# The weighted selection of a pair of experts, turned by 32x32 blocks on VectorE instead of by TensorE

## The chip, the cores and the metric

The kernel runs on one core of one Trainium2 chip. Its time is the device time of one launch in microseconds (us). Engines are named as the profile names them: PE is TensorE (PEld its weight loads), DVE is VectorE, ACT is ScalarE, POOL is GpSimd, SP is SyncE, which here only issues the loads of weights.

## What is computed

A trunk of four layers over 256 tokens of width 1024. Each layer has a token mixer (gated DeltaNet, differential attention, gMLP, DeltaNet again) and then a mixture of 16 experts of which every token takes two. The change lies in the experts alone:

```
for i in range(DEPTH):
    ...                                   # mixer, residual, layer norm
    m = grouped_moe(h, w_router, router_bias, e_w1[i], e_w3[i], e_w2[i])
    h = layer_norm(DN_ALPHA * h + m, ...)

def grouped_moe(x, ...):
    scores = sigmoid(t @ w_router)        # top 2 of the best group of 4 -> gates [256, 16]
    for e in range(N_EXPERTS):
        h = silu(t @ w1[e]) * (t @ w3[e]) # 1024 -> 512
        out = out + gates[:, e:e + 1] * (h @ w2[e])
```

All in float32.

## The kernel before

Each engine has one program written by hand, and the programs meet at semaphores; no scheduler moves anything. The experts of a layer are worked off in eight pairs, seven in a hardware loop and the last (`final`) in code of its own. For each expert up to 64 (`CAP`) of its tokens are picked; an expert with more gets extra passes under a branch (`PASSES`, `baton`).

`rank` on DVE gives each token, for each expert, its place among that expert's tokens (`place`), and `route` its gate (`gates`). A selection is a 0/1 matrix of 128 tokens by 64 slots, made by comparing `place` with the slot number `iota`. `sel` picks the tokens of a pair into `x_`; `selg` is the same with the gate in place of the 1 and brings the results back.

One pair on PE, in this order (function `pair` in the tensor block): `up` of expert 0 into bank 2 and of expert 1 into bank 3 (L1851, 32 matmuls each); `turn` of expert 0: `selg` of the first 128 tokens is transposed (L1858) and then the four pieces of `h_` (L1862), all into bank 2; `gather(0)` for the next pair (L1840, 16 matmuls); `turn` of expert 1, with `selg` of the other 128 tokens, into bank 3; `down` of both (L1869); `gather(1)`; and the four matmuls over `selgT` and `y_` that bring the pair's result back (L1968). The last pair has no gathers.

Around it ACT takes silu (L881) of each bank, copies the transposed selection into `selgT` (L891) and the transposed h into `hT` (L892), and copies `y_` (L897). DVE makes `selg` (L1365) and the next pair's `sel` (L1368), four operations of 128x64 each, taken in turn, at the start of the pair; then the product h of silu and the third matrix (L1374) for expert 0 and expert 1; then `pair_x` (L1343) and `pair_x_shift` (L1348), which scale and shift the gathered x; and adds the four banks of the result to H (L1421). At the start of a layer DVE makes the first `sel` (L1353) and both halves of the first `x_` before it enters the pairs. POOL then forms the scaled residual on H in four operations (L555, L561), in the time of the first pair.

What PE waits for, by bank: `free(b, n)` waits until bank b has been drained n times in this pair. DVE's product h counts as the first draining of bank 2 (expert 0) and of bank 3 (expert 1). Before, `free(2, 1)` and `free(3, 1)` stand directly ahead of the two turns.

SP loads the weights of a pair, six times 2 MiB, into a ring of six slots; a slot is loaded again when PE has passed its last reader (`weights_read`, counted up by the first instruction of expert 1's `up`, of expert 0's `turn`, of expert 1's `down` and of `gather(1)`).

## Time and profile before

| | |
|---|---|
| median of 3 runs | 2070.44 us (2067.48 to 2070.73) |
| profiled execution, its own time | 2060.59 us |
| its span | 2058.8 us |
| PE busy | 1866.4 us, 91% |
| DVE busy | 717.8 us, 35% |
| ACT busy | 502.1 us, 24% |
| POOL busy | 160.0 us, 8% |
| mean granted TensorE clock | 0.95 |
| moved by DMA | 504.47 MB, mean 245 GB/s |

The span is what the profiler sees from the first to the last instruction of the one profiled execution; some 1.8 us lie around it. In the rows below, a line of a timeline gives the start and the length in us, the engine, the line of the kernel, the operation, the tile written and the tiles read, their sizes and how many instructions were merged, and in brackets how long the engine stood idle before it and what ended that. "issue" there is time in which the engine waited for nothing that the profile shows.

### The profile page before, as it was taken

How to read it: one execution, taken by the hardware profiler on the slowest of the kernel's cores; microseconds unless marked ns; L12 is line 12 of the kernel's file. 1: busy time of each engine (PE TensorE's matmuls, PEld its weight loads, DVE VectorE, ACT ScalarE, POOL GpSimd, SP SyncE). 2: the span in 40 equal slices, each digit the busy share in tenths (PEclk: the TensorE clock that was granted, in tenths of full speed). 3: DMA queues.
4: the chain of work that ended last, by engine and by line, in shares of the span. 5: the costliest groups of instructions: out<-in, count | busy, mean ns of one | idle time of the engine just before them, and what ended most of it. 6: DMA issues, size and time to landing. Idle time of an engine off the chain costs nothing. (4 is left out here: it accounts for less than half of the span.)

```text
span 2058.8 us, 28401 instructions
## 1 busy us (share of the span) xinstructions
PE 1866.4 (91%) x10562; PEld 1024.9 (50%) x10563; DVE 717.8 (35%) x1433; ACT 502.1 (24%) x1006; POOL 160.0 (8%) x97
## 2 busy tenths in 40 slices
PE   7998979999895889889979998899989988899996
PEld 6867644443663444334434444434438768434442
DVE  2434453332305452223323115232323435443233
ACT  1664211221203111111111001122113845112211
POOL 1112021000300030000020002100002120020000
PEclk9999999999995899999999998999999999999999
DMA  9421159999741257548994424779994320279994
GB/s 353 143 83 64 42 198 408 429 426 400 269 149 41 82 228 293 209 192 368 428 346 152 163 82 169 301 320 426 421 401 146 123 103 3 82 302 428 424 426 176
DMA packets 80952, 504.47 MB, mean 245 GB/s; under 512 B 8195, under 2 KB 12340, under 8 KB 55996
## 3 DMA queue, kind: packets, MB, share of 16 engines
q1 hardware_dynamic: 69808, 488.65, 58.9%
q0 software_dynamic: 2304, 8.39, 1.2%
q10 hardware_dynamic: 8716, 5.66, 1.0%
q8 instruction: 92, 1.51, 0.3%
q14 instruction: 32, 0.26, 0.0%
HBM read 501.62 MB, written 1.06 MB: 244 GB/s over the span
## 5 line engine op out<-in xcount | busy, mean ns | idle before, releaser
L1851 PE MATMUL bank<-ring,work 128*64 128x512 f32 x2176 | 485.3, 604 | 12.0 <-DVE work L1388 6.0
L1851 PEld LDWEIGHTS bank<-ring,work 128*64 128x64 f32 x2176 | 156.0, 139 | 332.1 <-issue 324.7
L1869 PE MATMUL bank<-ring,work 128*64 128x512 f32 x1088 | 245.5, 602 | 7.5 <-ACT work L903 4.6
L1521 PE MATMUL bank<-HT,ring 128*128 128x256 f32 x1024 | 231.7, 386 | 4.3 <-DMA ring<-in_a_w_in 3.3
L1521 PEld LDWEIGHTS bank<-HT,ring 128*128 128x128 f32 x1024 | 198.3, 194 | 41.6 <-issue 11.5
L1529 PE MATMUL bank<-ring,HT 128*128 128x512 f32 x448 | 196.4, 598 | 0.0
L1374 DVE TENSOR_TENSOR work<-bank,work 64x512 f32<-64x512 f32 x64 | 68.1, 1064 | 325.5 <-ACT work L881 325.4
L881 ACT ACTIVATE work<-bank 64x512 f32<-64x512 f32 x64 | 37.7, 589 | 528.5 <-PE bank L1851 528.5
L1840 PE MATMUL bank<-work 128*128 128x128 f32 x1024 | 141.7, 296 | 11.0 <-DVE work L1353 7.2
L1869 PEld LDWEIGHTS bank<-ring,work 128*64 128x64 f32 x1088 | 76.7, 138 | 147.2 <-issue 139.7
L1840 PEld LDWEIGHTS bank<-work 128*128 128x128 f32 x1024 | 129.8, 206 | 36.4 <-issue 27.0
L1529 PEld LDWEIGHTS bank<-ring,HT 128*128 128x128 f32 x448 | 85.8, 193 | 104.3 <-issue 104.3
L1343 DVE TENSOR_TENSOR work<-bank,lncols 128x512 f32<-128x512 f32 x64 | 44.3, 692 | 261.9 <-PE bank L1840 261.9
L1968 PE MATMUL bank<-work 128*128 128x512 f32 x256 | 115.8, 595 | 9.4 <-issue 4.5
L897 ACT ACTIVATE work<-bank 64x512 f32<-64x512 f32 x128 | 75.8, 592 | 183.1 <-PE bank L1869 182.4
L1068 DVE SCALAR_TENSOR_TENSOR work<-bank,convcols,work 128x255 f32<-128x255 f32 x144 | 69.1, 481 | 108.3 <-ACT work L696 104.8
L1421 DVE TENSOR_TENSOR H<-bank,H 128x512 f32<-128x512 f32 x128 | 84.7, 686 | 58.6 <-PE bank L1968 58.3
L1554 PE MATMUL bank<-ring,work 128*128 128x512 f32 x192 | 84.9, 601 | 0.0
L1968 PEld LDWEIGHTS bank<-work 128*128 128x128 f32 x256 | 46.4, 191 | 59.2 <-issue 59.2
L558 POOL TENSOR_TENSOR H<-H,gB 128x1024 f32<-128x1024 f32 x6 | 14.0, 2356 | 751.6 <-PE bank L1512 751.6
L555 POOL TENSOR_TENSOR H<-work,gB 128x1024 f32<-128x1024 f32 x8 | 23.0, 2899 | 574.5 <-DVE work L1348 574.5
L1554 PEld LDWEIGHTS bank<-ring,work 128*128 128x128 f32 x192 | 36.5, 193 | 44.4 <-issue 44.4
(275 smaller groups left out, 1757.0 us busy)
## 6 DMA issues: line engine op xcount, KB each, us to landing
ring<-in_e_w SPq DMA_DIRECT2D x192, 2048.0 KB, 13.2
ring<-in_a_w_in SPq DMA_DIRECT2D x16, 2048.0 KB, 15.6
ring<-in_c_w_in SPq DMA_DIRECT2D x8, 2048.0 KB, 12.5
ring<-in_b_w_in SPq DMA_DIRECT2D x6, 2048.0 KB, 15.3
ring<-in_a_w_out SPq DMA_DIRECT2D x4, 2048.0 KB, 8.0
ring<-in_c_w_out SPq DMA_DIRECT2D x4, 2048.0 KB, 8.1
ring<-in_b_w_out SPq DMA_DIRECT2D x2, 2048.0 KB, 8.2
gB<-in_ln_mix_g POOLq DMA_DIRECT2D x4, 512.0 KB, 4.1
```

Of the source, the lines that this page charges most:

```text
L897: ins = a(y_[CAP * j:CAP * (j + 1), nh * 512:(nh + 1) * 512], bank[b][nh * CAP:(nh + 1) * CAP, :], ACT.Copy)
L1068: ins = v.scalar_tensor_tensor(dst[:, back:SEQ], ps[:, 0:SEQ - back], convcols[:, j, col:col + 1], dst[:, back:SEQ], ALU.mult, ALU.add)
L1343: v.tensor_tensor(sl, bank[g][:, :].rearrange("p (k c) -> p k c", k=4), lncols[:, g_col + 4 * g:g_col + 4 * g + 4].unsqueeze(2).to_broadca ...
L1374: v.tensor_tensor(by_m(h_[j]), bank[b][CAP:, :], sil[j][CAP:, :], ALU.mult).then_inc(drained[b], 1)
L1421: v.tensor_tensor(part(b), bank[b][:, :], part(b), ALU.add).then_inc(drained[b], 1)
L1521: ins = mm(dst[:, 0:SEQ], wt[:, k, n * P:(n + 1) * P], HT[:, k, :], start=k == 0, stop=k == KC - 1)
L1529: ins = mm(dst[:, :], HT[:, k, tt * P:(tt + 1) * P], wt[:, k, :], start=k == 0, stop=k == KC - 1)
L1554: ins = mm(ps[:, :], turned(h, tt), wts[nh][:, h, :], start=h == 0, stop=h == HEADS - 1)
L1840: ins = mm(bank[g][:, k * 2 * CAP:(k + 1) * 2 * CAP], XH[:, tt, (4 * g + k) * P:(4 * g + k + 1) * P], sel[:, tt, :], start=tt == 0, stop=t ...
L1851: ins = mm(bank[b][lo:lo + CAP, :], x[:, k, :], wt[:, k, :], start=k == 0, stop=k == KC - 1, skip_group_check=True)
L1869: ins = mm(bank[b][nh * CAP:(nh + 1) * CAP, :], h[:, m, :], w2[:, m, nh * 512:(nh + 1) * 512], start=m == 0, stop=m == 3, skip_group_check ...
L1968: mm(bank[b][:, :], selgT[:, tt * P:(tt + 1) * P], y_[:, nh * 512:(nh + 1) * 512], start=True, stop=True).then_inc(filled[b], 1)
```

## The change

The selection with gates is no longer made token by slot and transposed by PE. It is made slot by token in blocks of 32, so that a transpose within blocks, which DVE can do, gives `selgT`. For this each quarter of the partitions (32 of them) needs the places and gates of all four quarters. Once per layer 16 copies spread them over the quarters (`spread`, from `placed`, in which `place` and `gates` now lie side by side). In a pair DVE compares `slot_no` with the places (128x256), multiplies by the gates, makes the next `sel` as before (four operations), and transposes by blocks into `selgT`.

PE loses the two transposes of `selg` per pair, ACT the two copies into `selgT`. The wait for h of expert 0, `free(2, 1)`, moves from the turn into the middle of expert 1's `up`; the one for h of expert 1, `free(3, 1)`, moves ahead of the last matmul of `gather(0)`. The count of `sel_ready` is now given by DVE's transpose, and PE waits for it a second time before the last matmuls of the pair.

```diff
+                for a in range(4):
+                    for tb in range(4):
+                        out = spread[Q * a:Q * (a + 1), :, :].rearrange("p q (n t b) -> p t q n b", t=TT, b=4)
+                        ins = v.tensor_copy(out[:, :, :, :, tb], placed[Q * tb:Q * (tb + 1), :, :, a // 2:E:2])
+                ins.then_inc(spread_set, 1)
...
                 def pair(it, final):
-                    for tt in range(TT):
-                        for j in range(2):
-                            ins = v.tensor_scalar(selg[:, tt, CAP * j:CAP * (j + 1)], iota, place[:, tt, bass.ds(it * 2 + j, 1)],
-                                                  gates[:, tt, bass.ds(it * 2 + j, 1)], ALU.is_equal, ALU.mult)
-                            if not final:
-                                ins = v.tensor_scalar(sel[:, tt, CAP * j:CAP * (j + 1)], iota, place[:, tt, bass.ds(it * 2 + (j + 2), 1)], None, ALU.is_equal)
-                    ins.then_inc(sel_ready, 1)
+                    blocks = TT * P // Q
+                    at_b = [spread[:, q, bass.ds(it * blocks, blocks)].unsqueeze(2).to_broadcast([P, blocks, Q]) for q in range(2)]
+                    b3 = selb.rearrange("p (n c) -> p n c", c=Q)
+                    v.tensor_tensor(b3, slot_no.unsqueeze(1).to_broadcast([P, blocks, Q]), at_b[0], ALU.is_equal).then_inc(selb_step, 1)
+                    dve.wait_ge(selb_step, it * 2 + (E * i + 1))
+                    v.tensor_tensor(b3, b3, at_b[1], ALU.mult).then_inc(selb_step, 1)
+                    if not final:
+                        for tt in range(TT):
+                            for j in range(2):
+                                v.tensor_scalar(sel[:, tt, CAP * j:CAP * (j + 1)], iota, place[:, tt, bass.ds(it * 2 + (j + 2), 1)], None, ALU.is_equal)
+                    dve.wait_ge(selb_step, it * 2 + (E * i + 2))
+                    v.transpose(selgT, selb).then_inc(sel_ready, 1)
...
-                        a(selgT[:, j * P:(j + 1) * P], bank[b][:, 0:P], ACT.Copy)
                         a(hT[j], bank[b][:, SEQ:].rearrange("p (m c) -> p m c", m=4), ACT.Copy).then_inc(drained[b], 1)
...
-                        head, tail = up(2 + j, x_[:, :, CAP * j:CAP * (j + 1)], w1, w3, None if j else free)
+                        head, tail = up(2 + j, x_[:, :, CAP * j:CAP * (j + 1)], w1, w3, free, (2, 1) if j else (1, 0))
...
-                    free(2, 1)
-                    head, tail = turn(2, [selg[:, 0, :]], h_[0])
+                    head, tail = turn(2, [], h_[0])
...
-                        gather(0)[1].then_inc(filled[0], 1)
-                    free(3, 1)
-                    turn(3, [selg[:, 1, :]], h_[1])[1].then_inc(filled[3], 1)
+                        gather(0, free)[1].then_inc(filled[0], 1)
+                    else:
+                        free(3, 1)
+                    turn(3, [], h_[1])[1].then_inc(filled[3], 1)
...
+                    pe.wait_ge(sel_ready, it + ((E // 2 + 1) * i + 2))
                     free(2, 3)
```

On DVE, at the entry into the loop of the pairs, from its first operation to the product h of expert 0 (`work` holds both `selg` or its blocks and `sel`; ISA and REGISTER_ALU rows set addresses). Before:

```order
L1365 TENSOR_SCALAR work<-consts_sb,place,gates 128x64
L1368 ISA
L1368 TENSOR_SCALAR work<-consts_sb,place 128x64
...
L1365 TENSOR_SCALAR work<-consts_sb,place,gates 128x64
L1368 ISA
L1368 TENSOR_SCALAR work<-consts_sb,place 128x64
L1370 REGISTER_ALU
L1370 TENSOR_LOAD counts
...
L1374 TENSOR_TENSOR work<-bank2,work 64x128x4
```

After:

```order
L1378 TENSOR_TENSOR work<-consts_sb,spread 128x256
L1379 ISA
L1380 ISA
L1380 TENSOR_TENSOR work<-work,spread 128x256
L1384 ISA
L1384 TENSOR_SCALAR work<-consts_sb,placed 128x64
...
L1384 TENSOR_SCALAR work<-consts_sb,placed 128x64
L1386 STREAM_TRANSPOSE work<-work 128x256
...
L1391 TENSOR_TENSOR work<-bank2,work 64x128x4
```

Four gated selections became two products and a transpose; the four plain ones stand together behind the products, and all of it still precedes the product h.

On PE, from expert 1's up-projection (bank 3) through the two turns, in the loop of the pairs, with the semaphores waited for. Before:

```order
L1851 MATMUL bank3<-ring1,work 64x512
L1851 MATMUL bank3<-ring0,work 64x512
L1851 MATMUL bank3<-ring1,work 64x512
...
L1858 MATMUL bank2<-consts_sb,work 128x128 [waits drained2]
L1862 MATMUL bank2<-consts_sb,work 128x64 x4
L1926 REGISTER_ALU
L1840 MATMUL bank0<-work 128x128 [waits sel_ready]
L1840 MATMUL bank0<-work 128x128 x7
L1858 MATMUL bank3<-consts_sb,work 128x128 [waits drained3]
L1862 MATMUL bank3<-consts_sb,work 128x64 x4
```

After:

```order
L1870 MATMUL bank3<-ring1,work 64x512
L1906 REGISTER_ALU
L1870 MATMUL bank3<-ring0,work 64x512 [waits drained2]
L1870 MATMUL bank3<-ring1,work 64x512
...
L1880 MATMUL bank2<-consts_sb,work 128x64 x4
L1944 REGISTER_ALU
L1859 MATMUL bank0<-work 128x128 [waits sel_ready]
L1859 MATMUL bank0<-work 128x128 x6
L1859 MATMUL bank0<-work 128x128 [waits drained3]
L1880 MATMUL bank3<-consts_sb,work 128x64 x4
```

The two transposes of 128x128 are gone, the wait for bank 2 stands in the up-projection, and the wait for bank 3 inside the gather.

## Rows read from the trace of the kernel before

**Rows 1.** Timeline of PE, a settled pair of layer 0 in the loop.

```profile
344.00 13.95 PE L1851 MATMUL bank<-ring,work 128*64 128x512 f32 x64
357.88 0.33 PE L1858 MATMUL bank<-consts_sb,work 128*128 128x128 f32 x1
358.14 0.46 PE L1862 MATMUL bank<-consts_sb,work 64*128 64x64 f32 x4
358.53 2.05 PE L1840 MATMUL bank<-work 128*128 128x128 f32 x16
360.42 0.27 PE L1858 MATMUL bank<-consts_sb,work 128*128 128x128 f32 x1
360.62 0.46 PE L1862 MATMUL bank<-consts_sb,work 64*128 64x64 f32 x4
```

**Rows 2.** Windows, the next pair: busy by engine, then PEclk, DMA share, GB/s.

```profile
373.44:402.89 29.45, 29.45 (x148) 12.65 (x147) 8.99 (x18) 5.93 (x11) 0.00 (x0) 1.00 1.01 428
```

**Rows 3.** Timeline of DVE, first pair of layer 0.

```profile
277.17 0.69 DVE L1343 TENSOR_TENSOR work<-bank,lncols 128x512 f32<-128x512 f32 x1 [3.87 <-PE bank L1840]
...
281.31 0.31 DVE L1365 TENSOR_SCALAR work<-consts_sb,place,gates 128x64 f32<-128x64 f32 x1
...
281.69 2.86 DVE L1365 TENSOR_SCALAR work<-consts_sb,place,gates 128x64 f32<-128x64 f32 x1
...
287.51 2.34 DVE L1368 TENSOR_SCALAR work<-consts_sb,place 128x64 f32<-128x64 f32 x1
289.76 2.38 DVE L1365 TENSOR_SCALAR work<-consts_sb,place,gates 128x64 f32<-128x64 f32 x1
...
292.34 1.07 DVE L1374 TENSOR_TENSOR work<-bank,work 64x512 f32<-64x512 f32 x1
```

**Rows 4.** Timeline of POOL in the same stretch.

```profile
281.57 5.75 POOL L555 TENSOR_TENSOR H<-work,gB 128x1024 f32<-128x1024 f32 x2 [105.10 <-DVE work L1348]
287.40 4.70 POOL L561 TENSOR_TENSOR H<-H,bB 128x1024 f32<-128x1024 f32 x2
```

**Rows 5.** Timeline of PE, first and last pair of layer 0.

```profile
279.87 14.02 PE L1851 MATMUL bank<-ring,work 128*64 128x512 f32 x64
...
304.22 3.65 PE L1869 MATMUL bank<-ring,work 128*64 128x512 f32 x16 [2.74 <-issue]
...
500.34 8.78 PE L1851 MATMUL bank<-ring,work 128*64 128x512 f32 x32 [2.03 <-issue]
...
510.89 0.33 PE L1858 MATMUL bank<-consts_sb,work 128*128 128x128 f32 x1 [1.11 <-DVE work L1374]
```

**Rows 6.** Two lines by source: shortest/median/longest in ns, first and last start.

```profile
L1130 DVE TENSOR_TENSOR HT<-work,consts_sb x40: 413/424/2556, 158.6 to 1732.4; 128x256 f32<-128x256 f32 x40
...
L1106 DVE COPY egl<-work x8: 171/172/433, 125.6 to 1667.7; 128x8 f32<-128x8 f32 x8
```

**Rows 7.** Timeline of DVE in the settled pair of rows 1.

```profile
351.75 1.07 DVE L1374 TENSOR_TENSOR work<-bank,work 64x512 f32<-64x512 f32 x1 [5.35 <-ACT work L881]
...
358.62 1.07 DVE L1374 TENSOR_TENSOR work<-bank,work 64x512 f32<-64x512 f32 x1 [5.80 <-ACT work L881]
```

**Rows 8.** Timeline of PE and DVE, first pair of layer 3.

```profile
1803.23 13.95 PE L1851 MATMUL bank<-ring,work 128*64 128x512 f32 x64
...
1815.73 1.07 DVE L1374 TENSOR_TENSOR work<-bank,work 64x512 f32<-64x512 f32 x1
```

**Rows 9.** Timeline of POOL and DVE, two places where both work in SBUF.

```profile
159.41 4.83 POOL L584 TENSOR_TENSOR work<-work,angb 128x1024 f32<-128x1024 f32 x2 [14.59 <-ACT work L722]
...
160.51 4.02 DVE L1130 TENSOR_TENSOR HT<-work,consts_sb 128x256 f32<-128x256 f32 x2 [1.11 <-PE bank L1625]
...
310.63 2.77 POOL L543 TENSOR_SCALAR gB<-gB 128x1024 f32<-128x1024 f32 x1 [17.11 <-DMA bB<-in_ln_ffn_b]
...
311.94 0.69 DVE L1348 TENSOR_TENSOR work<-work,lncols 128x512 f32<-128x512 f32 x1
```

**Rows 10.** DMA issues from 358.5 to 360, median us to landing.

```profile
ring<-in_e_w SPq DMA_DIRECT2D x2, 2048.0 KB, 15.0
```

More of the change, by code:

```diff
@@ L59 @@
 C_FOLD = C_IOTA + 2 * CAP
-C_SB = C_FOLD + E
+C_SLOT = C_FOLD + E
+Q = 32
+C_SB = C_SLOT + Q
 C_OH = C_SB
@@ L229, in trunk @@
         tri = K_[:, C_TRI:C_TRI + P]
+        slot_no = K_[:, C_SLOT:C_SLOT + Q]
         fold = K_[:, C_FOLD:C_FOLD + E]
@@ L256, in trunk @@
         rs = sb("rs", [P, 4, TT])
-        gates = sb("gates", [P, TT, E])
-        place = sb("place", [P, TT, PASSES * (E + 2)])
+        placed = sb("placed", [P, TT, 2, PASSES * (E + 2)])
+        place, gates = placed[:, :, 0, :], placed[:, :, 1, 0:E]
+        spread = sb("spread", [P, 2, E // 2 * TT * P // Q])
         counts = ctx.enter_context(nc.sbuf_tensor("counts", [1, E], mybir.dt.int32))
@@ L317, in trunk @@
         logitT = work[:, 6144:6144 + SEQ]
+        selb = work[:, 2304:2560]
         iota2 = K_[:, C_IOTA:C_IOTA + 2 * CAP]
@@ L322, in trunk @@
         pairs = work[:, 8704:9216]
-        sel, selg, selgT = view(2048, TT, 2 * CAP), view(2304, TT, 2 * CAP), work[:, 2560:2816]
+        sel, selgT = view(2048, TT, 2 * CAP), work[:, 2560:2816]
         x_ = view(2816, KC, 2 * CAP)
@@ L357, in trunk @@
         sel_ready = sem("sel_ready")
+        spread_set = sem("spread_set")
+        selb_step = sem("selb_step")
         silu_h = sem("silu_h")
@@ L1304, in route @@
                 own.link(v.reciprocal(rs[:, 2, :], rs[:, 1, :]))
-                own.link(v.tensor_tensor(gates[:, :, :], V3(5), rs[:, 2, :].unsqueeze(2).to_broadcast([P, TT, E]), ALU.mult))
+                own.link(v.tensor_tensor(gates, V3(5), rs[:, 2, :].unsqueeze(2).to_broadcast([P, TT, E]), ALU.mult))
             def rank(i):
@@ L1359, in experts @@
                     pair_x_shift(g)
+                dve.wait_ge(spread_set, i + 1)
                 def pair(it, final):
[L1363 to L1369 removed]
+                    blocks = TT * P // Q
[10 more added lines that the diff above has]
+                    v.transpose(selgT, selb).then_inc(sel_ready, 1)
                     counted = [dve.value_load(counts[0:1, bass.ds(it * 2 + j, 1)], min_val=0, max_val=SEQ) for j in range(2)]
@@ L1834, in experts, with gather @@
                 done(mm(ps[:, 2 * E:3 * E], ones[:, :], mask[1], start=False, stop=True, skip_group_check=True), "rank", i)
-                def gather(g):
+                def gather(g, later=None):
                     for k in range(4):
                         for tt in range(TT):
+                            if later is not None and (k, tt) == (3, TT - 1):
+                                later(3, 1)
                             ins = mm(bank[g][:, k * 2 * CAP:(k + 1) * 2 * CAP], XH[:, tt, (4 * g + k) * P:(4 * g + k + 1) * P], sel[:, tt, :],
@@ L1843, in gather, with up @@
                     return head, ins
-                def up(b, x, w1, w3, later=None):
+                def up(b, x, w1, w3, later=None, then=None):
                     for k in range(KC):
                         if later is not None and k == KC // 2:
-                            later(1, 0)
+                            later(*then)
                         for lo, wt in ((0, w1), (CAP, w3)):
@@ L1857, in turn @@
                     for n, tile in enumerate(columns):
-                        ins = tr(bank[b][:, n * P:(n + 1) * P], tile, ident)
-                        head = ins if n == 0 else head
+                        tr(bank[b][:, n * P:(n + 1) * P], tile, ident)
                     for m in range(4):
@@ L1862, in turn @@
                         ins = tr(bank[b][:, c:c + CAP], h[CAP:, m * P:(m + 1) * P], ident[CAP:, CAP:])
+                        head = ins if m == 0 else head
                     return head, ins
@@ L2043, in constants @@
     c[:, C_CD + E:C_CD + 2 * E] = (other > mine).reshape(1, E)
+    c[:, C_SLOT:C_SLOT + Q] = m // Q * Q % CAP + np.arange(Q)[None, :]
     c[:, C_IOTA:C_IOTA + 2 * CAP] = np.arange(2 * CAP) % CAP
```

## The prediction, made before the changed kernel was run

> **What bounds the kernel now.** I read the page first: PE is by far the busiest engine, so the question is where PE waits and what it does in between. The timeline of PE in a settled pair of the expert loop answers it for the largest part: from 344.00 on every row starts where the last one ended [rows 1], the next pair starts at 373.44 [rows 2], so a pair takes 29.44 us, and PE is never idle in it. So in those stretches the time is the sum of PE's instructions, and whatever leaves PE leaves the time, provided nothing else becomes late. The next view is the one of windows: in such a pair the DMA engines are busy all the time and move 428 GB/s [rows 2]. The six loads of a pair are 6 x 2 MiB = 12.58 MB, so PE and DMA run neck and neck. What is not settled is the first pair of each layer. There the timeline of DVE shows selection instructions of 64 columns that take 2.3 to 2.9 us instead of 0.3 [rows 3], exactly while POOL runs its four operations on H [rows 4]. Before the change nobody pays for that. PE asks for h of expert 0 only at its first transpose.
>
> **What leaves PE.** Two 128x128 transposes per pair. Their cost is the distance to the next start: 358.14 - 357.88 = 0.26 and 360.62 - 360.42 = 0.20, together 0.46 us [rows 1]. Four layers have 28 pairs in the loops: 28 x 0.46 = 12.9. In the last pair of a layer there is no gather between the two turns, and in layer 0 PE waits 1.11 us for h of expert 1 before the second turn [rows 5]. Taking 0.26 away ahead of that wait only lengthens it, so such a pair yields 0.20. I count two layers so, and two with 0.46, since there PE stands still earlier and h is ready: 1.3. Sum: 14.2 us off PE.
>
> **What leaves ACT** (two copies of 128x128 a pair) lies beside PE's work. It brings the copies of hT 0.2 to 0.3 earlier, and PE does not wait for them in a settled pair [rows 1]: nothing.
>
> **What DVE gets in a settled pair.** Four selections with a gate go, two products of 128x256 and one blockwise transpose of 128x256 come. A product of that size takes 0.42 (L1130) [rows 6]. For the transpose no row exists: the nearest is the same 0.42, and I bound it from 0.3 to 1.2. Before the product h of expert 0 at 351.75, 7.75 us into the pair, DVE stood idle for 5.35 [rows 7]: the selection was done 2.4 us in. One us more hides there: nothing. The gather now waits for a signal given after the transpose, some 3 to 4 us into the pair, and comes to it at 14.3: nothing. The wait for h of expert 1 moves in front of the gather's last matmul. The sixteen matmuls take 360.42 - 358.53 = 1.89 [rows 1]; with the 0.26 gained they start 14.27 us into the pair, the last at 16.04. h of expert 1 is ready at 358.62 + 1.07 = 359.69, 15.69 us in [rows 7]: a margin of 0.3 us, nothing, but this is the thinnest place.
>
> **What DVE gets once per layer.** Sixteen copies of 32 partitions between the first selection and the first product of x. DVE stands idle there for 3.87 us, ahead of 277.17 [rows 3]. A copy of eight columns (L1106) takes 0.17 [rows 6]; one after the other that is 2.8, with 0.2 each 3.2. Hidden, by the gather on PE. If they took over 0.3 each, some tenths of a us per layer would show.
>
> **The wait that moves.** This is the term that decides. PE now asks for h of expert 0 not at the turn but in the middle of expert 1's up-projection, after 48 of the 64 matmuls. These take 357.88 - 344.00 = 13.88, so the point lies 10.41 us into the pair. In a settled pair h is ready at 7.75 + 1.07 = 8.8 [rows 7]. In the first pair of layer 0, which PE starts at 279.87 [rows 5], the point falls on 290.28, and DVE starts the product h only at 292.34 and needs 1.07: it is ready at 293.41 [rows 3]. So even with DVE exactly as before PE would stand still for 3.1 us, where it now has 0.4 to spare. In layer 3: 1803.23 + 10.41 = 1813.64 against 1815.73 + 1.07 = 1816.80, again 3.2 [rows 8]. Layers 1 and 2 show the same distances within 0.05. Queued behind this wait is the rest of the up-projection, both turns and everything later in the pair; all of it moves.
>
> How does the new code change DVE's lateness? In the rows, one selection gets through at the end of each POOL operation, and the last waits until the fourth has ended at 292.10 [rows 3, 4]. The first product (comparison with the slots) starts ahead of POOL and runs free. The second, by the gates, must wait for the first and so falls under POOL. It reads two tensors from SBUF. L1130 is such an operation: mostly 0.42, but 2.56 at the longest [rows 6], and two of them together take 4.02 from 160.51, under two POOL tensor_tensor on work that begin at 159.41 [rows 9]. Against it stands L1348 at 311.94, also with two SBUF inputs, 0.69 as elsewhere, in the middle of a POOL operation that begins at 310.63 [rows 9]; but that one is a tensor_scalar, and the four here are tensor_tensor [rows 4]. I go by L1130: the product waits for POOL's first operation. Then four selections follow, one or two per POOL operation, the last one again until about 292.2, then the transpose (0.42), then h (1.07): ready at about 293.8. PE stands still for 3.5 us. Four layers: 14.0. The lower bound is that neither the product nor the transpose waits for POOL: then the fourth selection is through at 289.8 (as the row at 287.51 plus its length would be), h is ready at 291.4, and the stall is 1.1. The upper bound has a transpose of 1.2 that waits too: 4.4.
>
> The Trainium skill (SBUF — State Buffer, "Who interferes with whom") says that a DVE instruction with two SBUF inputs contends with a GpSimd instruction that reads SBUF, and that the one which issues first holds the pair to its end. L1130 agrees, L1348 beside the tensor_scalar does not. By the rule the stall is 3.5 and the time 2073.5; were it wrong here, 1.1 and about 2062.
>
> **The clock.** After an idle stretch the 32 matmuls of an up-projection took 8.78 instead of about 7.1 (idle 2.03 before them), while after 2.74 idle 16 matmuls took the usual 3.65 [rows 5]. The stall is longer than both. I charge 1.7 us in two layers of four: 3.4; bounds 0 and 6.8.
>
> **The loads.** A pair of 28.98 us wants 12.58 MB / 28.98 = 434 GB/s, and 428 was moved with the engines full [rows 2]. If 428 is the ceiling, loads fall back 0.4 us per pair, 2.5 to 3 over a layer. The load issued about 359 lands 15.0 later, at 374 [rows 10], and is wanted by expert 1's up-projection of the next pair, which starts half of 13.88 into it, at 373.44 + 6.94 = 380.4: 6 us in hand, and the stall gives the queue 3.5 more. Nothing, but not certain. The Trainium skill (DMA: Bandwidth & Descriptors) names 435 GB/s as the ceiling of the SBUF side; by it 28.98 us would just be fed.
>
> **Sum**, against the profiled execution's own 2060.6: - 14.2 + 14.0 + 3.4 = 2063.8, that is 3.2 more. That execution is 9.8 below the median of the runs, 2070.4, so the median becomes about 2073.5.
>
> **Rivals.**
> - *A short stall.* Product and transpose slip past POOL: 4 x 1.1 + 1.7 for one fall of the clock - 14.2 = -8.1, time 2062.3. For it: L1348's row. Against: L1130's. 0.17.
> - *No stall worth naming*, PE only loses its transposes: 2056.2. It needs DVE through by 290.3, which no row supports. 0.05.
> - *The moved wait costs more than the transposes* (the slower side): the blockwise transpose takes 1.2 and waits for POOL as well, and PE's clock falls each time: 4 x (4.4 + 1.7) - 14.2 = +10.2, time 2080.6. It decides from a stall of some 3.6 with the clock falling in three layers on. For it: the longest idle stretch in the rows that ended in a fall is shorter than this one. 0.17.
> - *The loads become the bound*: pairs stay at 29.4, so only 1 to 3 us of the 14.2 arrive: about +15, time 2085. For it: full DMA engines. Against: 6 us in hand. 0.05.
>
> **How the numbers follow.** The forecast holds 0.56, around 2073.5, give or take 4 for the clock and for code arriving late at other places (idle rows ended by "issue", as the 2.03 and 2.74 us in [rows 5]; the code of the pair is rearranged). A measurement of this kernel can tell about 0.2%, 4.1 us. Of the forecast's 0.56 some 0.02 lies below -4.1 and 0.20 above +4.1. Faster: 0.17 + 0.05 + 0.02 = 0.24; slower: 0.17 + 0.05 + 0.20 = 0.42; same: 0.34. The range from 2062 to 2081 takes in the short stall and the long one and leaves out the two ends.
>
> **What would show it.** In the trace of the changed kernel: settled pairs of 28.98 us without idle PE; in each first pair an idle stretch of PE about 10.4 us in, released by DVE's product h, 3.5 long in the forecast, 1.1 in the first rival; the gate product of 128x256 at 2.5 to 3 us there and 0.42 elsewhere. Idle PE released by DMA on ring in late pairs would mean the loads. The prediction is wrong if h of expert 0 is ready before PE reaches the middle of the up-projection, or if the settled pair does not shrink by 0.46.

## The result, and the profile after

The changed kernel took 2076.17 us in the median of 20 runs (2065.52 to 2087.28), the kernel before 2065.73 in the median of 20 runs interleaved with them (2056.26 to 2074.73). The ratio is 1.0049, with a 95% interval of 1.0034 to 1.0063. That is 10.1 us more, where the prediction said 3.2 more. The profiled execution of the changed kernel has a span of 2074.2 us and a mean granted TensorE clock of 0.944 (before: 2058.8 and 0.95).

A settled pair in the loop, on the timeline of PE (start and length in us, engine, line, what it writes and reads, how many instructions). It answers to [rows 1]; up is now L1870, the turn L1880, the gather L1859, down L1888, the matmuls that bring the result back L1988:

```profile
769.21 13.95 PE L1870 MATMUL bank<-ring,work 128*64 128x512 f32 x64
783.10 0.46 PE L1880 MATMUL bank<-consts_sb,work 64*128 64x64 f32 x4
783.49 2.05 PE L1859 MATMUL bank<-work 128*128 128x128 f32 x16
785.47 0.46 PE L1880 MATMUL bank<-consts_sb,work 64*128 64x64 f32 x4
785.86 7.09 PE L1888 MATMUL bank<-ring,work 128*64 128x512 f32 x32
...
798.29 1.08 PE L1870 MATMUL bank<-ring,work 128*64 128x512 f32 x4
```

The two transposes of the selection are gone, PE is still never idle, and the pair takes 798.29 - 769.21 = 29.08 us instead of 29.44. No wait on a DMA appears in any pair.

The first pair of a layer, here of layers 0 and 1, on the same timeline. The bracket is idle time before the row and what ended it; these rows answer to the first of [rows 5]:

```profile
278.22 10.77 PE L1870 MATMUL bank<-ring,work 128*64 128x512 f32 x48
292.08 6.54 PE L1870 MATMUL bank<-ring,work 128*64 128x512 f32 x16 [3.09 <-DVE work L1391]
...
736.56 10.52 PE L1870 MATMUL bank<-ring,work 128*64 128x512 f32 x48
750.43 3.65 PE L1870 MATMUL bank<-ring,work 128*64 128x512 f32 x16 [3.35 <-DVE work L1391]
```

After 48 of the 64 matmuls PE stands still until DVE's product h of expert 0 (L1391). The list of PE's waits (total us, times, longest) gives the sum over the four layers:

```profile
PE bank L1870 <- DVE work L1391: 13.1, 4, 3.4
```

Why h is late stands on the timelines of DVE and POOL in the first pair of layer 1 (answering to [rows 3, 4]):

```profile
730.82 3.20 DVE L1364 COPY spread<-placed 32x32 f32<-32x32 f32 x16
734.77 0.69 DVE L1349 TENSOR_TENSOR work<-bank,lncols 128x512 f32<-128x512 f32 x1 [0.75 <-PE bank L1859]
...
738.00 0.41 DVE L1378 TENSOR_TENSOR work<-consts_sb,spread 128x256 f32<-128x256 f32 x1
738.57 2.86 DVE L1380 TENSOR_TENSOR work<-work,spread 128x256 f32<-128x256 f32 x1 [0.15 <-DVE work L1378]
741.35 7.60 DVE L1384 TENSOR_SCALAR work<-consts_sb,placed 128x64 f32<-128x64 f32 x4
748.88 0.43 DVE L1386 STREAM_TRANSPOSE work<-work 128x256 f32<-128x256 f32 x1
749.34 1.04 DVE L1391 TENSOR_TENSOR work<-bank,work 64x512 f32<-64x512 f32 x1
...
738.26 5.91 POOL L562 TENSOR_TENSOR H<-work,gB 128x1024 f32<-128x1024 f32 x2 [180.21 <-DVE work L1354]
744.25 4.66 POOL L568 TENSOR_TENSOR H<-H,bB 128x1024 f32<-128x1024 f32 x2
```

The gate product (L1380) takes 2.86 us instead of 0.42, the four plain selections 7.60 together, and they end at 748.95, as POOL's fourth operation does (744.25 + 4.66 = 748.91). The block transpose (0.43) and the product h (1.04) follow, and PE goes on at 750.43. The sixteen copies that spread places and gates take 3.20 us once per layer and lie beside the gather on PE: DVE still stands idle for 0.75 after them.

### The profile page after: what moved, and what is told of

Same layout as the page of the kernel before. It is cut to its first block and busy times, and to the rows that moved or that the text cites. A ratio compares the mean times of both kernels' runs of the same rounds, so it can differ in the third digit from the quotient of the medians.

```text
span 2074.2 us, 28227 instructions
## 1 busy us (share of the span) xinstructions
PE 1871.9 (90%) x10498; PEld 1023.6 (49%) x10499; DVE 735.9 (35%) x1465; ACT 491.1 (24%) x942; POOL 160.7 (8%) x97
## 5 line engine op out<-in xcount | busy, mean ns | idle before, releaser
L1870 PE MATMUL bank<-ring,work 128*64 128x512 f32 x2176 | 494.2, 612 | 22.8 <-DVE work L1391 13.1
L1870 PEld LDWEIGHTS bank<-ring,work 128*64 128x64 f32 x2176 | 158.0, 141 | 349.2 <-issue 325.3
L1888 PE MATMUL bank<-ring,work 128*64 128x512 f32 x1088 | 249.8, 610 | 8.9 <-ACT work L909 4.6
L1391 DVE TENSOR_TENSOR work<-bank,work 64x512 f32<-64x512 f32 x64 | 67.8, 1060 | 332.8 <-ACT work L888 332.7
L1888 PEld LDWEIGHTS bank<-ring,work 128*64 128x64 f32 x1088 | 77.1, 140 | 152.3 <-issue 145.0
L1859 PE MATMUL bank<-work 128*128 128x128 f32 x1024 | 139.7, 294 | 7.4 <-DVE work L1359 6.8
L1859 PEld LDWEIGHTS bank<-work 128*128 128x128 f32 x1024 | 128.3, 204 | 32.8 <-issue 23.7
L1988 PE MATMUL bank<-work 128*128 128x512 f32 x256 | 117.3, 602 | 9.5 <-ACT work L903 5.2
L1988 PEld LDWEIGHTS bank<-work 128*128 128x128 f32 x256 | 46.7, 193 | 60.3 <-issue 60.3
## 6 DMA issues: line engine op xcount, KB each, us to landing
ring<-in_e_w SPq DMA_DIRECT2D x192, 2048.0 KB, 13.3
```

The costliest lines, as they stand in the source:

```text
L1391: v.tensor_tensor(by_m(h_[j]), bank[b][CAP:, :], sil[j][CAP:, :], ALU.mult).then_inc(drained[b], 1)
L1859: ins = mm(bank[g][:, k * 2 * CAP:(k + 1) * 2 * CAP], XH[:, tt, (4 * g + k) * P:(4 * g + k + 1) * P], sel[:, tt, :], start=tt == 0, stop=t ...
L1870: ins = mm(bank[b][lo:lo + CAP, :], x[:, k, :], wt[:, k, :], start=k == 0, stop=k == KC - 1, skip_group_check=True)
L1888: ins = mm(bank[b][nh * CAP:(nh + 1) * CAP, :], h[:, m, :], w2[:, m, nh * 512:(nh + 1) * 512], start=m == 0, stop=m == 3, skip_group_check ...
L1988: mm(bank[b][:, :], selgT[:, tt * P:(tt + 1) * P], y_[:, nh * 512:(nh + 1) * 512], start=True, stop=True).then_inc(filled[b], 1)
```

## The experiments

Each batch of four shared one chip and its own runs of the kernel before: 23 runs for the first batch (median 2064.59 us), 35 for the second (2063.60), 24 for the third (2064.0; one more, of 9476 us, is left out). "Pair" is the time from one start of up to the next on PE's timeline.

**1. The moved wait alone.** The kernel before, with only the wait for h of expert 0 where the change puts it:

```
-  head, tail = up(2 + j, ..., w1, w3, None if j else free)
+  head, tail = up(2 + j, ..., w1, w3, free, (2, 1) if j else (1, 0))
   ...
-  free(2, 1)
   head, tail = turn(2, ...
```

> The kernel before, with only the wait for h of expert 0 moved into the middle of expert 1's up-projection; selection and transposes as before. Theory: the old selection is held up by POOL just as long, h is ready 13.5 us into the first pair, so PE stands still for 3.1 us in each of four layers, 12.5 in all, and the clock falls in about half of them (1.7 to 3 us each): ratio 1.007 to 1.009. Rival (the stall needs the new products and the transpose on DVE): no stall, ratio 1.000.

Measured: 2080.27 us, ratio 1.0078 (1.0049 to 1.0106), so 16 us slower with no other edit. Its list of waits:

```profile
PE bank L1851 <- DVE work L1374: 11.8, 4, 3.0
```

The stall does not need the new work on DVE. The lateness of h is there in the kernel before too, and costs nothing only because PE asks for h 3.5 us later.

**2. The hold by POOL.** The changed kernel, with POOL's operations on H held until that h is made:

```
   wait_copy(pool, "first", i, 1)
+  pool.wait_ge(drained[2], at[("moe", i)][2] + 1)
```

> The changed kernel, but POOL begins its four operations on H in the first pair only when h of expert 0 is done. Theory (POOL holds DVE up): the gate product of the first pair takes 0.42 instead of 2.85, the four selections 0.74 instead of 7.6, h is ready 8.8 us in and PE does not stall at the unchanged wait: ratio 0.995. What could take it back: POOL's operations now lie beside the scaling of the next pair's x, whose second part reads two SBUF tensors and may be held up to 2.9 us; that has some 12 us of room. Rival (DVE is late by its own work or by the code it has to fetch): the stall stays, ratio 1.005.

Measured: 2061.25 us, ratio 0.9984 (0.9966 to 1.0003). The gate product, by source (shortest, median and longest of 32 in ns), is never long:

```profile
L1381 DVE TENSOR_TENSOR work<-work,spread x32: 424/425/428, 284.7 to 2017.3; 128x256 f32<-128x256 f32 x32
```

In the changed kernel the same line reads 424/424/2861. No wait at up is left. The mechanism is as expected, the gain is less than the 0.995 expected. In this trace the pairs are shorter by 9.1 us than in the mean of the two profiles of the kernel before, with a loss in layer 1 that is told under 8 already in it. Outside of them the mixer of layer 3 took more, which is told under 9.

**3. DVE's order.** The changed kernel, with the next pair's four plain selections made after the product h of expert 0 instead of before:

```
-  if not final: v.tensor_scalar(sel[...], iota, place[...], None, ALU.is_equal)   # x4
   dve.wait_ge(selb_step, ...)
   v.transpose(selgT, selb)
   ...
   v.tensor_tensor(by_m(h_[j]), bank[b][CAP:, :], sil[j][CAP:, :], ALU.mult).then_inc(drained[b], 1)
+  if j == 0 and not final: v.tensor_scalar(sel[...], ...)                         # x4
```

> The changed kernel, but DVE makes the next pair's plain selections after the product h of expert 0 instead of ahead of it; waits and POOL as in the change. Theory (h is late because five instructions queue ahead of it under POOL): only the gate product is held (2.85), the transpose is through 5 us in, h waits for silu alone and is ready at 8.8; no stall, ratio 0.995, while POOL is as long as before. Rival (the wait in the middle of the accumulation costs by itself): an idle stretch stays there, ratio near 1.005.

Measured: 2059.78 us, ratio 0.9975 (0.9955 to 0.9996): this kernel beats both. POOL still works at the old time here, so the first pair of layer 1 shows which of DVE's operations it holds:

```profile
733.56 2.86 DVE L1380 TENSOR_TENSOR work<-work,spread 128x256 f32<-128x256 f32 x1
736.45 0.45 DVE L1382 STREAM_TRANSPOSE work<-work 128x256 f32<-128x256 f32 x1
739.31 1.09 DVE L1389 TENSOR_TENSOR work<-bank,work 64x512 f32<-64x512 f32 x1 [2.41 <-ACT work L888]
740.43 3.87 DVE L1393 TENSOR_SCALAR work<-consts_sb,placed 128x64 f32<-128x64 f32 x4
...
733.25 5.90 POOL L562 TENSOR_TENSOR H<-work,gB 128x1024 f32<-128x1024 f32 x2 [181.58 <-DVE work L1354]
739.23 4.69 POOL L568 TENSOR_TENSOR H<-H,bB 128x1024 f32<-128x1024 f32 x2
```

The product of two tensors in SBUF is held (2.86), and the four selections are, 3.87 instead of some 0.74. The transpose (0.45) and the product h (1.09), which take one tensor from SBUF, run at full speed in the middle of POOL's work. The Trainium skill (SBUF — State Buffer, "Who interferes with whom") names the port pair that VectorE and GpSimd share, held by one of them at a time. The rows of the product, of the transpose and of h agree. The selections are held as well, though they read one tensor and a column of places. In the changed kernel itself the transpose never met POOL, since it starts when POOL ends.

The same trace has a row that bears on the prediction's reading of L1348, which took its usual 0.69 beside a tensor_scalar of POOL. Its twin L1354 did not, 0.21 us after POOL's tensor_scalar had begun at 311.73:

```profile
311.94 1.36 DVE L1354 TENSOR_TENSOR work<-work,lncols 128x512 f32<-128x512 f32 x1
```

In experiments 7 and 1 it began 0.38 and 0.57 us after such an operation and took 1.20 and 1.01. In all three it ended 1.6 us after POOL's start. Where it began before POOL's operation, or 1.0 us or more after its start, it took 0.69. So a tensor_scalar of POOL (2.77 us) holds such a product too, but only in its first 1.6 us. The four operations of the first pair are tensor_tensor and hold to their end, so the forecast did not depend on this.

Experiment 3 has a price of its own: an expert with more than 64 tokens needs the selections of its extra pass right behind the product h, and these now queue behind the plain ones. PE's wait for them grew from 10.9 us (longest 2.7) to:

```profile
PE bank L1936 <- DVE work L1403: 12.2, 4, 3.4
```

**4. The wait later.** The changed kernel, with the wait for h of expert 0 ahead of the last matmul of expert 1's up:

```
-  if later is not None and k == KC // 2:
+  if later is not None and k == KC // 2 and then[0] == 1:
       later(*then)
   for lo, wt in ((0, w1), (CAP, w3)):
+      if later is not None and (k, lo) == (KC - 1, CAP) and then[0] == 2:
+          later(*then)
```

> The changed kernel, but PE asks for h of expert 0 ahead of the last of the 64 matmuls of the two up-projections instead of after 48. Theory (the stall at the moved wait is the loss): in the changed kernel h is ready 13.8 us into the first pair, PE comes to the new place at 13.7, so the four stalls of 3.1 to 3.4 us shrink to 0.2 each, and no fall of the clock follows them. Settled pairs stay at 29.08. Time: ratio to the kernel before 0.995, some 10 us below it (0.36 x 28 for the transposes) and some 20 below the changed kernel. Rival (the new DVE work or the waits inside PE's matmuls cost the time, wherever they stand): ratio stays near 1.005.

Measured: 2079.46 us, ratio 1.0076 (1.0048 to 1.0105). This was a miss. The 3 us stall was gone, and another kind of idle time stood in its place. PE and DVE in the first pair of layer 1:

```profile
735.12 14.95 PE L1872 MATMUL bank<-ring,work 128*64 128x512 f32 x64
756.20 0.69 PE L1882 MATMUL bank<-consts_sb,work 64*128 64x64 f32 x4 [6.13 <-issue]
...
747.89 1.05 DVE L1391 TENSOR_TENSOR work<-bank,work 64x512 f32<-64x512 f32 x1
```

h is ready at 748.94, up ends at 750.07 (1.0 later than its usual 13.95, for which the short wait at its last matmul does not account), and PE then waits 6.13 us for nothing that the profile shows. Layer 3 has 5.05 at the same place, and all such "issue" gaps together are 37.9 us, against 20.7 in the changed kernel and 26.0 before. The DMA view of stretches (queue and kind: packets, MB, share of 16 engines) has the reason. The queue named q8 instruction brings pieces of 16 KB. Of the 64 "issue" gaps over 0.4 us in the first pairs of all fourteen traces, 54 end 2.2 to 2.75 us after the start of such a piece (the others up to 4.7), so I read it as PE's code. From 741 to 753 us (the first three lines) no piece comes, and between 753 and 754 (the last line) there is one:

```profile
q1 hardware_dynamic: 218, 3.31, 71.9%
q0 software_dynamic: 31, 0.13, 2.6%
q14 instruction: 1, 0.01, 0.2%
...
q8 instruction: 1, 0.02, 6.1%
```

In the kernel of experiment 2 pieces came 8.0 and 14.4 us after the start of up, at 742.0 and 748.4. In this one neither came. The next was at 753.5, 4.6 us after h had released the wait, and PE went on 2.7 later. In layer 3 of the changed kernel it is alike: the wait was released at 1832.3, a piece came at 1836.3, and a gap of 2.83 ended at 1838.75. It holds in every trace: in the 20 first pairs in which the wait held PE (the changed kernel twice, experiments 1, 4 and 10) the first piece after h came 3.7 to 4.6 us after h was ready, 17.4 to 18.7 us after the start of up. In the other 36 first pairs the piece of that place came at 13.3 to 15.4 us.

**5. Is it the lateness or the place?** Experiments 3 and 4 together: the wait at its late place, but h ready long before.

> The changed kernel with VectorE making the next pair's plain selection only behind expert 0's h product, and with TensorE's wait for that product put ahead of the last matmul of expert 1's up instead of the middle. It tells apart why the late wait alone kept the time at 1.008 with 6.13 and 5.05 us of idle ahead of the turn in layers 1 and 3. Theory A (the wait held TensorE's queue until the product came, and the next piece of its code was asked for only then): here the product is ready some 6 us before the wait is reached, nothing is held, the third piece of code lands 6 to 8 us after the start of up as in the kernel with the early product, no idle over 3 us stands ahead of the turn, and the ratio is that of the early product with the wait in the middle, 0.9975 (0.996 to 0.999). Theory B (the wait instructions at that place shift the code, and a piece now begins ahead of the turn): the idle of 5 to 6 us stays, up lasts 14.9 and not 13.95 us, ratio 1.003 to 1.006.

Measured: 2062.9 us, ratio 0.9985 (0.9967 to 1.0003). PE in the first pair of layer 1:

```profile
732.76 13.95 PE L1875 MATMUL bank<-ring,work 128*64 128x512 f32 x64
746.65 0.46 PE L1885 MATMUL bank<-consts_sb,work 64*128 64x64 f32 x4
747.04 2.05 PE L1862 MATMUL bank<-work 128*128 128x128 f32 x16
```

No gap, up back at 13.95, and the third piece of code at 740.2, 7.4 us after the start of up. In layers 2 and 3 a gap of 2.2 us stands ahead of the turn, as in layer 3 of the kernel before (2.39), and none over 3. The place is harmless. What costs is that a wait which really holds PE also holds the request for its next code, and at the end of up there is nothing left to cover its arrival. The wait in the middle at least has 16 matmuls (3.65 us) behind it. One thing the rows leave open: why the piece at about 8 us is missing in layer 1 of experiment 4 and in layer 2 here. It was due well before the wait. I take its absence for the other part of the 6.13 us, but no run shows that by itself.

**6. What a transpose is worth.** Experiment 3 with one 128x128 transpose put back into each turn (its result is read by nobody, and ACT copies nothing):

```
-  head, tail = turn(2, [], h_[0])
+  head, tail = turn(2, [selb[:, 0:P]], h_[0])
   ...
-  turn(3, [], h_[1])[1].then_inc(filled[3], 1)
+  turn(3, [selb[:, P:2 * P]], h_[1])[1].then_inc(filled[3], 1)
```

> The changed kernel with the plain selection behind expert 0's h product, and with one 128-row transpose put back ahead of each of the two turns (of the selection that is made on VectorE; nothing reads the result, and ScalarE copies nothing). TensorE does what it did before, VectorE what it does after. Theory (two transposes are worth 0.36 us in a settled pair, 28 of them): settled pair 29.45 again, 10 us over the same kernel without them (2059.8), ratio to before 1.002 to 1.003. Rival (the transposes' time is partly covered or the clock gives it back): settled pair under 29.3, ratio under 1.000.

Measured: 2066.56 us, ratio 1.0024 (1.0012 to 1.0036), 0.0049 above experiment 3. That is 10.1 us, give or take 5 by the two intervals, and 28 x 0.36 is 10.1 too. A settled pair is back at 29.45, with the gather between the turns in 1.89 us:

```profile
359.69 0.46 PE L1883 MATMUL bank<-consts_sb,work 64*128 64x64 f32 x4
360.08 2.05 PE L1862 MATMUL bank<-work 128*128 128x128 f32 x16
361.97 0.27 PE L1880 MATMUL bank<-consts_sb,work 128*128 128x128 f32 x1
362.17 0.46 PE L1883 MATMUL bank<-consts_sb,work 64*128 64x64 f32 x4
```

**7. Where 0.09 us of it went.** In the changed kernel that gather takes 785.47 - 783.49 = 1.98 us. The kernel before, with only the wait for h of expert 1 moved in front of the gather's last matmul:

```
+  if later is not None and (k, tt) == (3, TT - 1):
+      later(3, 1)
   ins = mm(bank[g][:, k * 2 * CAP:(k + 1) * 2 * CAP], ...
   ...
-  gather(0)[1].then_inc(filled[0], 1)
-  free(3, 1)
+  gather(0, free)[1].then_inc(filled[0], 1)
```

> The kernel before with only the wait for expert 1's h product moved from ahead of its turn to ahead of the last matmul of the next pair's first gather. Theory A (the 0.09 us that this gather is longer in the changed kernel, 1.98 against 1.89 in a settled pair, comes from the wait inside it): gather 1.98 here, settled pair 29.54. Theory B (it comes from what stands around it, a 64-row transpose next to a matmul of 128 rows, now that no 128-row transpose lies between): gather 1.89 as before, settled pair 29.45. Ratio 0.999 to 1.002 in both.

Measured: 2063.89 us, ratio 1.0011 (0.9990 to 1.0031), and the gather unchanged:

```profile
360.06 2.05 PE L1842 MATMUL bank<-work 128*128 128x128 f32 x16
361.95 0.27 PE L1860 MATMUL bank<-consts_sb,work 128*128 128x128 f32 x1
```

So the wait costs nothing. In the settled pairs of all fourteen traces the gather takes 1.98 when a transpose of 64 rows follows it and 1.89 when one of 128 rows does; experiment 6 has the wait inside the gather and still 1.89. What PE does in these 0.09 us the rows do not show.

**8. Does the place in the middle cost by itself?** Experiment 1 with POOL held as in experiment 2:

> The kernel before with the wait for expert 0's h product in the middle of expert 1's up (1.0078 by itself) and with GpSimd's residual multiplies of each layer's first pair held until that product is made. Theory A (the move costs by the stall alone, and the stall is GpSimd's hold on VectorE): no wait at up, every plain and gate-weighted selection at its undisturbed length, ratio 0.999 to 1.001. Theory B (the place of the wait costs by itself, by code that comes later or by the clock): no wait at up either, but ratio over 1.003.

Measured: 2061.9 us, ratio 0.9991 (0.9968 to 1.0015). So without the stall nothing of the 1.0078 of experiment 1 is left that can be measured.

Its trace, and those of experiments 2, 3 and 6, also show where a part of the gain stays away. In layer 1 two neighbouring pairs have experts with more than 64 tokens, three extra passes in all. PE's timeline of that stretch has, in the kernel before and in the changed one (L1914 and L1933 are the gather of an extra pass):

```profile
829.40 4.65 PE L1914 MATMUL bank<-work 128*128 128x64 f32 x32 [2.72 <-DVE work L1383]
```

```profile
834.25 7.09 PE L1933 MATMUL bank<-work 128*128 128x64 f32 x32 [2.72 <-DVE work L1400]
```

The same wait, the same 32 matmuls, 4.65 us before and 7.09 after (4.72 and 6.95 in the third pass, 5.72 and 5.45 in the first). The windows over that whole stretch, the two overflowing pairs up to the next up (length, busy time of PE, PEld, DVE, ACT and POOL, PEclk, DMA share, GB/s), first of before, then of after:

```profile
793.45:933.17 139.72, 120.49 (x575) 54.26 (x575) 35.60 (x69) 17.22 (x31) 0.00 (x0) 0.91 0.52 208
```

```profile
798.29:943.69 145.40, 126.12 (x572) 58.75 (x571) 36.01 (x67) 16.54 (x27) 0.00 (x0) 0.87 0.48 193
```

The granted clock is 0.87 instead of 0.91: more of the stretch runs at the lower of the two levels (1.2 GHz) after the same waits. In both kernels the clock falls three times in it, once at each extra pass's wait, for 10.2, 6.8 and 6.8 us before and for 10.2, 13.7 and 13.7 after. The stretch takes 139.7 us in the kernel before and in experiment 7, and 143.0 to 147.9 in all the others, which all have their own lengths of the first pair or of a wait.

**9. Both cures at once.** Experiments 2 and 3 together:

> The changed kernel with both cures: the plain selection behind expert 0's h product, and GpSimd's multiplies of the residual held until that product is made. Theory A (each takes the same 3.3 us stall away, so the two together give no more than one): ratio 0.997 to 0.9985, no wait at up, gate product 0.42 us in every pair. Theory B (GpSimd also slows something else in the first pair that TensorE waits for): first pairs of layers 0 and 3 (33.6 and 35.75 with the first cure alone) shorter by 1 us and more, ratio under 0.996.

Measured: 2058.71 us, ratio 0.9973 (0.9957 to 0.9989). The two remove the same stall, and together give no more than one. The first pairs of layers 0 and 3 took 34.18 and 35.38 us, against 33.60 and 35.75, so theory B finds no support either.

The traces also show a second place where a part of the gain stays away. The stretch from the last up of layer 2 to the first up of layer 3, most of it the mixer of layer 3, has the same mixer code in every kernel. It took 298.6 to 302.1 us (mean 300.0) in the six traces in which PE makes the transposes, and 300.8 to 307.7 (mean 304.8) in the eight in which it does not. Length times what the granted clock lacks to 1 was 15.1 us in the mean of the six and 19.9 in that of the eight, which is the whole difference. Why it falls more there is open.

**10. A longer hold.** The changed kernel, with the gate product done twice (the first time into columns that nobody reads):

```
+  if not final:
+      v.tensor_tensor(<256 free columns>, b3, at_b[1], ALU.mult)
   v.tensor_tensor(b3, b3, at_b[1], ALU.mult).then_inc(selb_step, 1)
```

> The changed kernel with the gate product done twice in every pair but the last of a layer, the first time into columns that nothing reads. In the first pair of a layer each costs 2.85 us while GpSimd works, elsewhere 0.42. Theory A (VectorE's lateness in the first pair goes to TensorE one for one): the stall grows from 3.3 to 6.1 us in each of 4 layers, 11.4 us in all, settled pairs stay at 29.08, and with what the clock takes the ratio to before is 1.011 to 1.014. Theory B (the longer stall overlaps time in which TensorE would wait for code anyway): stall 6.1, but ratio under 1.009.

Measured: 2077.43 us, ratio 1.0065 (1.0042 to 1.0089). Both theories were wrong in the stall, which grew to 3.5 to 3.74 and not to 6.1. DVE and POOL in the first pair of layer 1:

```profile
735.16 2.86 DVE L1381 TENSOR_TENSOR work<-work,spread 128x256 f32<-128x256 f32 x1 [0.15 <-DVE work L1378]
737.93 3.09 DVE L1382 TENSOR_TENSOR work<-work,spread 128x256 f32<-128x256 f32 x1
740.95 4.97 DVE L1386 TENSOR_SCALAR work<-consts_sb,placed 128x64 f32<-128x64 f32 x4
745.84 0.43 DVE L1388 STREAM_TRANSPOSE work<-work 128x256 f32<-128x256 f32 x1
...
740.83 4.71 POOL L568 TENSOR_TENSOR H<-H,bB 128x1024 f32<-128x1024 f32 x2
```

The second product takes 3.09 and the selections 2.6 less than in the changed kernel (4.97 against 7.60). DVE gets one such operation through per operation of POOL (a selection of 0.24 us can slip in between two of them), and once POOL is done (745.54) the rest runs free. The lateness of h is therefore POOL's end plus what is left, not the sum of the queued operations: with five of them queued h is ready 1.5 us after POOL's end, with six 1.8.

**11 and 12. The same two kernels once more,** to see what varies between executions.

> The kernel before, unchanged, profiled once more, to see how far the clock's falls lie alike in two executions. Theory A (they do): clock losses of the four expert stages 2.5, 12.9, 8.2 and 2.4 us again, within the 1.6 that two digits leave, and layer 1's five overflow pairs 139.7 us. Theory B (they vary from one execution to the next): layer 1's overflow pairs up to 145, as in every kernel with a changed first pair but one.

> The changed kernel, unchanged, profiled once more and timed beside the others. Theory A (the stall's clock falls belong to the kernel): the 16 matmuls behind the stall take 6.5 us in layers 0 and 2 and 3.65 in layers 1 and 3 again. Theory B (they vary): other layers fall. The stall itself is 3.1 to 3.35 us in each layer in both; ratio 1.0035 to 1.0065.

Measured, before: 2067.2 us, span 2065.4. The stretch of layer 1, which the expectation calls five pairs (it has five starts of up, in two pairs), took 139.68 us:

```profile
793.20:932.88 139.68, 120.45 (x577) 54.85 (x576) 35.59 (x69) 17.20 (x31) 0.00 (x0) 0.91 0.52 209
```

The losses to the clock in the four stages (length times what PEclk lacks to 1) were 2.5, 12.9, 11.0 and 4.8 us, so the first two came again and the last two did not. After: 2073.61 us in 8 runs, ratio 1.0045 (1.0025 to 1.0065), the stretch 145.40 us as before. The stall was there again:

```profile
PE bank L1870 <- DVE work L1391: 13.2, 4, 3.3
```

The 16 matmuls behind it took 3.65, 3.65, 6.61 and 5.35 us in layers 0 to 3, where the first profile had 6.54, 3.65, 6.66 and 3.65. Which layers lose the clock behind the stall varies; the loss in the stretch of layer 1 did not in these two executions of each kernel.

## Why the prediction was right, and in which step it was not

The time lies on the side that the prediction held likeliest and inside its range; its size, +10.1 against +3.2 us, does not come out of the sum. Two executions of each kernel are profiled, and their pairs add up, from the first up to the last up of each layer, to 948.0 and 950.8 us before and 961.5 and 956.4 after: +9.5 in the mean. Where two numbers stand in a field, they are of the first and of the second profiles. By steps:

| step | predicted | measured |
|---|---|---|
| transposes in 28 pairs | -12.9 (0.46 each) | -10.1 (0.36 each) |
| transposes in last pairs (outside the 9.5; from the first turn to down) | -1.3 | -0.27, -0.43, -0.20, -0.21: -1.1 |
| stall at the moved wait | +14.0 (4 x 3.5) | +13.1 and +13.2 |
| clock behind the stall | +3.4 (2 x 1.7) | +5.9 and +4.7 |
| code that arrives late, in first pairs | not counted | -3.9 and -2.3 |
| clock in layer 1's overflowing pairs | not seen | +6.4 |
| clock elsewhere in the pairs | not seen | -2.3 in the mean |
| copies of ACT, spread, loads | 0 | 0 |

The three rows on the clock come from one sum: the length of the pairs times what the granted clock lacks to 1 was 18.8 and 25.6 us before, 34.1 and 29.0 after, +9.4 in the mean. With the means the column, without the last pairs, comes to -10.1 + 13.2 - 3.1 + 9.4 = +9.4, where the timelines give +9.5. The two profiles of one kernel differ by 2.8 and 5.1 us, so a single row of the clock is not known to better than that, except the one of the overflowing pairs, which came out alike twice.

Part of the agreement is luck. The prediction added its sum to 2070.4, the median of three runs; twenty runs put the kernel before at 2065.73. From there its sum gives 2068.9, and its range ends at 2076.3, where 2076.17 was measured. And +10.1 is nearly the +10.2 of the rival in which the moved wait costs more, but not by that rival's mechanism: it wanted a block transpose of 1.2 us that POOL holds and a fall of the clock behind every stall. The transpose took 0.43 and started when POOL had ended, and the clock fell behind two stalls of four.

- **The stall** was right in place, in what releases it, and within 0.4 us in size, with the gate product held (2.86) and the block transpose not (0.43 to 0.45). Experiments 1, 2 and 8 show that moving the wait causes all of it and that POOL's hold on DVE is the reason. That h was late already before, by 3.1 us against the new place, was in the rows [rows 3]; experiment 1 confirms it with 2.75 to 3.05. Experiment 10 shows what sets its length: the end of POOL's chain plus the rest, as in the prediction's own count (last selection at about 292.2), and not a sum of held operations.
- **The transposes** were over-sized. The step that failed took the distances to the next start as the whole saving [rows 1]. It did not ask what the neighbours cost once the transpose between them is gone; the gather gives back 0.09 of 0.46. The 0.10 us per pair, over 28 pairs, are 2.8 of the 6.9 us by which the sum fell short; most of the rest is the clock.
- **The clock** was under-sized. A fall cost 1.7 to 3.0 us per 16 matmuls, not 1.7, and the prediction looked only behind the new stall. The larger part, 5.7 us more in layer 1's overflowing pairs where 0.7 less was due (two pairs of 0.36), lies in a stretch that the change hardly touches. There the waits of 2.7 us stood before and after (the two rows of experiment 8), but the clock stayed low longer behind them.
- **Code that arrives late** took something off. First pairs had 11.1 us of "issue" gaps before (layer 0: 4.4, as the 2.74 in [rows 5]) and 7.2 after in the first profiles, 8.2 and 5.9 in the second. Experiment 1, whose only edit is the moved wait, has 5.2. I read this as a part of the stall lying where PE would have waited for code anyway; no run tests that by itself.
- **The loads, ACT's copies and the sixteen copies** cost nothing, as said. The copies took 3.20 us, the upper of the two figures worked out.

From kernel to kernel the medians fit this account, each ratio being known to 0.0012 to 0.0024. Without a stall the change is worth 0.9975 (experiment 3). Its transposes alone are worth 0.0049 (experiment 6). So the rest of the edit, with experiment 3's own price of 1.3 us, costs 0.0024, about 5 us. In the traces layer 1's pairs alone have 6.0 of it (286.96 us before, 292.99 in experiment 6). The stall, with all that hangs on it, takes the ratio from 0.9975 to 1.0049, about 15 us (give or take 5) for 13.1 of standing still.

What stays open: why the clock stays low longer in the overflowing pairs of nearly every variant, and in the mixer of layer 3 of those without the transposes. Experiment 8 has the very instructions of the kernel before in the overflowing pairs, and is 8 us longer in them; but it was profiled once, in an execution 8.5 us above the median of its own runs. The kernel before and the changed one were profiled twice and repeat there within 0.05 us, so it is not chance from one execution to the next in these two. No run here varies one distance ahead of the stretch alone, so nothing more can be said of the cause.

## What to carry to other kernels

Before a wait is moved forward, compare the time of its new place with the time at which its producer is ready in the worst iteration, not in the settled one; here the first pair of a layer had 0.4 us to spare at the old place and lacked 3.1 at the new one. Then order the producing engine's work by who is waited for: making the next pair's selections after the product that PE wants turned +0.49% into -0.25% (0.9955 to 0.9996). And a gain of 0.5% on PE can be offset by the clock in a stretch that the edit does not touch, so compare stage by stage over two executions before believing a sum.

## What the runs showed of the hardware

- Beside GpSimd's tensor_tensor operations on SBUF, VectorE gets about one operation through per operation of theirs, if it is a product of two tensors in SBUF (128x256: 2.86 to 3.09 us instead of 0.42) or a selection against a column of places (128x64: 2.3 to 2.9 instead of 0.25). A block transpose of 128x256 (0.45) and a product with one operand in PSUM (1.09) are not held. Beside a tensor_scalar of GpSimd (128x1024, 2.77 us) a product of two tensors in SBUF is held only until 1.6 us after that one's start (1.01 to 1.36 us instead of 0.69).
- A block transpose of 128x256 float32 on VectorE took 0.43 to 0.45 us, and a copy of 32x32, most of them from one quarter of the partitions to another, 0.18 to 0.19.
- A wait that holds TensorE also holds what brings its next 16 KB of code. In 20 of 20 such first pairs the piece came 3.7 to 4.6 us after what was waited for was ready, and most idle stretches of "issue" in first pairs (54 of 64) ended 2.2 to 2.75 us after the start of such a piece. A wait of some 0.2 us at the end of up was so followed by 5 to 6 us of idle time in two layers of four.
- A gather of 16 matmuls that is followed by a transpose of 64 rows takes 0.09 us longer than one followed by a transpose of 128 rows.
